# Second block of a two-block transformer kernel: head norms by one root and one reciprocal, residual rows from the norm's rows, context masks on TensorE

## The chip, the cores and the metric

The kernel runs on one core of a Trainium2 chip. The metric is the device time of one execution in microseconds. All arithmetic is fp32. Times named as places (1401.62, say) are microseconds from the start of the profiled span.

## What is computed

Two transformer blocks of two layers each run one after the other over 256 tokens of width 1024. The first has differential attention, a convolution and a mixture of 16 experts, and ends each layer with a layer norm (gain `ln2_g`, bias `ln2_b`). Its output `x` goes into the second block, which the change touches. There 256 context tokens run beside the 256 tokens; the last layer no longer updates the context. The part that matters, cut:

```python
h = rms_norm(x, g_mix[l]) * (1 + sc1) + sh1          # tokens; the same for the context
qa, ka, va, fb, qc, kc, vc = jnp.split(h @ w_in, ...)
qa = rms_norm(qa.reshape(b, l, 6, 64), q_norm)       # head norm: only qa and ka
ka = rms_norm(ka.reshape(b, l, 2, 64), k_norm)
qa, ka, qc, kc = rope of each                        # tokens only
o = concat([global_attention(qa, ka, va, ctx),       # all 512 keys
            fourier_mix(fb),
            window_attention(qc, kc, vc, ctx, sink)]) # |key - query| <= 128, context keys, a sink logit
x = x + gt1 * (o @ w_out[l])
x = x + gt2 * swiglu(...)
```

`rms_norm` over a head is y / sqrt(mean of y squared over 64 channels + 1e-6), times a gain.

## The kernel before, in words

`build` writes one instruction stream per engine by hand: SP loads weight tiles of 2 MB into a ring of six slots, PE (TensorE) multiplies, ACT (ScalarE) and DVE (VectorE) read PSUM. Engines wait for one another on counting semaphores; each engine's order is the order of its program text, so an instruction that waits holds everything behind it on that engine. PSUM has eight banks of 128 x 512.

The first block keeps its rows token-major in `acc`. At the end of its last layer DVE's `row_norm` and ACT's `row_norm` normalise the halves of the rows (L2172, L1635), PE turns them in `turned_rows`, and DVE and ACT write the turned chunks, with gain and bias, into `X` (feature-major, L2179, L1642). PE then multiplies the context's half of the first projection (`context_chunk`) and sums the squares of `X`; DVE's `rms(T, 4, 0, 8, 4)` and ACT's `modulate` make the normalised `h2`.

The second block's loop over the layers `l` (0 and 1) begins on PE with the projection: twelve chunks `n` of 128 output features, each 8 products of 128x128 by the tokens (256 columns, or 512 for chunks 3, 8 and 9 in layer 1). Chunks 0 to 2 are the six qa heads in pairs, 3 is ka, 4 is kc, 5 to 7 are qc, 8 and 9 the values, 10 and 11 the Fourier input. ACT copies each into `pj` and squares chunks 0 to 3 into `squares_h` (L2004). Behind chunk 4 PE sums the squares over each head's 64 channels: `norm_sums` with the block matrix `mean_h`, a 128x128 matrix, once for each of the four chunks, into banks 4 and 5 in turn. The sum comes out copied onto all 64 partitions of its head. DVE adds eps and moves it to SBUF (`variance`, L2085), ACT takes the root (L1622), and DVE takes the reciprocal (`inverse`, L2090) and multiplies (L2997), chunk after chunk: four reciprocals of 128x512 in layer 0. Then DVE rotates chunks 0 to 7 (L3002, L2079, L3005), and signals `s_rope` after chunks 3 and 7.

In layer 0 only, PE turns the tokens' half of `X` back into rows (16 transposes into banks 2, 3, 6 and 7), and ACT copies them into `XR`, the same memory seen as residual rows (L2025).

The attention loop goes over units `(kind, hp, qb, ...)`: kind 0 is global, kind 1 banded; `hp` a pair of heads; `qb` a block of 128 queries. Blocks 0 and 1 are tokens and see 512 keys (four blocks, 1024 columns for the pair), blocks 2 and 3 are context queries and see 256. Layer 0 has 24 units, layer 1 has 12 (no context queries). Step `s` on PE: scores of unit `s` as two products of 64 rows each (after the exponentials of unit s - 2), transposes of the probabilities of unit s - 2 (L1548), the product with the values of unit s - 3. On DVE: the mask addition for banded token queries (L3024, PSUM in place), the negated row maximum (L3027), for kind 1 the sink's part (L3030 and L3032), then reciprocal and scaling of unit s - 1 (L3040, L3044) and the copy of the heads of unit s - 3 (L3054). On ACT: the copy of the transposes (L2039), two exponentials with row sums (L2044) and for kind 1 one exponential of the two sink columns (L2047). Two Fourier steps stand at units 0 and 1. The order in which one PE unit is built:

```python
for par in range(2):
    ins = mm(banks[:, SCORE_BANKS[s % 2] + par, 0:n * P], pj[r, Q_AT[kind] + hp, qb * P:qb * P + P],
             keys[r, k0 * P:(k0 + n) * P], start=True, stop=True)
ins.then_inc(s_scores, 1)
```

Every matrix product of the kernel goes through the helper `mm` (L556), all DMAs of weights through `tile` (L387).

## Time and profile before

| | |
|---|---|
| median of three executions | 2317.36 us (2317.27 to 2323.43) |
| profiled execution, its own time | 2318.68 us |
| its span in the profile | 2317.0 us |
| mean granted TensorE clock | 0.986 of full |
| busy: PE, DVE, ACT, POOL | 2229.0, 1186.2, 448.6, 3.5 us |
| second block, layer 0, projection to last unit | about 1339 to 1482 us |
| second block, layer 1, the same | about 1960 to 2068 us |

A timeline row gives the start, the duration (of a run of equal instructions taken together), the engine, the line, the operation, its operands, the count, and in brackets how long the engine sat idle before it and what ended that. A matrix product in fp32 appears as two records. An engine whose busy share is high is not by that the bound: where another engine's instruction stands between its own, that one is.

### The profile page before, as it was taken

What the parts mean: (1) busy time and instruction counts of PE and PEld (TensorE: products, weight loads), DVE (VectorE), ACT (ScalarE), POOL (GpSimd) and SP (SyncE); (2) the same over time, 40 slices, a digit from 0 to 9 for tenths busy, and PEclk for the clock granted to TensorE, in tenths of its full rate; (3) what the DMA queues carried; (4) which work ended last, traced back from release to release, by engine and by line L of the source; (5) the groups of instructions that cost most, each with busy time, mean ns of one, the idle gap of its engine ahead of it and who ended that gap; (6) DMA issues with size and microseconds to landing.
All of it is one profiled execution on the core that took longest, in us unless ns stands there. A gap on an engine that the chain in (4) does not pass through costs nothing.

```text
span 2317.0 us, 24671 instructions
## 1 busy us (share of the span) xinstructions
PE 2229.0 (96%) x9725; PEld 1399.2 (60%) x9725; DVE 1186.2 (51%) x1983; ACT 448.6 (19%) x1013; POOL 3.5 (0%) x23
## 2 busy tenths in 40 slices
PE   8999999999989999999999998899999999998998
PEld 7755445544357754445444785678888887554453
DVE  3755874211157267752111357765556433687666
ACT  1001402211111014022111225320000102352010
POOL 0000000000000000000000000000000000000000
PEclk9999999999999999999999999999999999999999
DMA  8345844799953459346999520002212124403340
GB/s 337 146 175 224 363 172 173 306 423 428 428 229 146 151 201 412 118 168 272 423 428 427 231 92 18 1 1 102 81 73 87 59 92 172 155 10 145 136 172 18
DMA packets 35983, 451.41 MB, mean 195 GB/s; under 512 B 5160, under 2 KB 7066, under 8 KB 8474
## 3 DMA queue, kind: packets, MB, share of 16 engines
q1 hardware_dynamic: 32992, 447.63, 47.7%
q10 hardware_dynamic: 2874, 2.17, 0.3%
q8 instruction: 81, 1.33, 0.2%
q14 instruction: 36, 0.29, 0.0%
HBM read 448.73 MB, written 1.05 MB: 194 GB/s over the span
## 4 chain that ended last, share of the span: by engine, by line
PE 77%; DMA 10%; DVE 8%; DVEq 2%; issue 1%; ACT 1%; SPq 0%; ACTq 0%
PE banks L556 74%; DMA ring<-in_w_exp_up 9%; PE banks L1548 1%; DVE tiny L3027 1%; DVEq L2091 1%; PE banks L707 1%; DVE tiny L2370 1%; DMA ring<-in_w_in 1%; DVE arena L2384 1%; DVE arena L2090 1%; DVE arena L3044 0%; DVE arena L2079 0%; DVE ring L2116 0%; DVE banks L2367 0%; DVE ring L2825 0%
## 5 line engine op out<-in xcount | busy, mean ns | idle before, releaser
L556 PE MATMUL banks<-ring,arena 128*64 128x512 f32 (+2 forms) x3290 | 966.2, 554 | 18.6 <-DMA ring<-in_w_exp_up 5.8
L556 PEld LDWEIGHTS banks<-ring,arena 128*128 128x128 f32 (+1 forms) x3290 | 446.8, 167 | 506.7 <-issue 473.6
L556 PE MATMUL banks<-arena 128*128 128x128 f32 (+6 forms) x1568 | 239.7, 346 | 13.6 <-ACT arena L2044 6.9
L556 PE MATMUL banks<-X,ring 128*128 128x256 f32 x1024 | 224.1, 381 | 1.8 <-DMA ring<-in_w_in 1.2
L556 PEld LDWEIGHTS banks<-X,ring 128*128 128x128 f32 x1024 | 195.8, 192 | 30.9 <-issue 3.3
L556 PEld LDWEIGHTS banks<-arena 128*128 128x128 f32 (+2 forms) x1568 | 154.5, 176 | 72.3 <-issue 31.5
L556 PE MATMUL banks<-arena,ring 128*128 128x256 f32 (+1 forms) x736 | 178.0, 399 | 2.4 <-ACT arena L1873 2.3
L556 PEld LDWEIGHTS banks<-arena,ring 128*128 128x128 f32 x736 | 139.6, 190 | 36.3 <-issue 17.3
L2215 DVE TENSOR_TENSOR arena<-arena,banks 128x512 f32<-128x512 f32 x16 | 11.0, 687 | 258.2 <-ACT arena L1696 258.2
L556 PE MATMUL banks<-ring 128*128 128x256 f32 x616 | 137.0, 380 | 0.0
L2116 DVE TENSOR_TENSOR ring<-ring 128x2048 f32<-128x2048 f32 (+1 forms) x56 | 119.7, 2138 | 18.0 <-ACT arena L1658 12.5
L556 PEld LDWEIGHTS banks<-ring 128*128 128x128 f32 x616 | 117.3, 190 | 16.0 <-issue 0.5
L2825 DVE TENSOR_TENSOR ring<-ring 128x2048 f32<-128x2048 f32 (+2 forms) x40 | 85.3, 2132 | 32.7 <-PE banks L556 15.0
L556 PE MATMUL banks<-ring,X 128*128 128x512 f32 x192 | 85.1, 593 | 0.3 <-ACT wsums L1614 0.3
L556 PE MATMUL banks<-arena,wsums 128*128 128x256 f32 x320 | 72.3, 379 | 0.0
L556 PEld LDWEIGHTS banks<-arena,wsums 128*128 128x128 f32 x320 | 60.9, 190 | 8.1
L556 PE MATMUL banks<-ring,wsums 128*128 128x256 f32 (+1 forms) x224 | 64.2, 441 | 0.3 <-DVEq L2117 0.3
L556 PEld LDWEIGHTS banks<-ring,X 128*128 128x128 f32 x192 | 36.3, 191 | 43.6 <-issue 43.5
L2198 DVE TENSOR_TENSOR arena<-arena,banks 128x512 f32<-128x512 f32 x64 | 43.9, 686 | 33.7 <-PE banks L556 33.7
L2218 DVE TENSOR_TENSOR arena<-arena,banks 128x512 f32<-128x512 f32 x16 | 11.0, 688 | 96.8 <-PE banks L556 96.8
L1614 ACT ACTIVATE arena<-banks 128x256 f32<-128x256 f32 (+1 forms) x60 | 26.0, 439 | 173.7 <-PE banks L556 170.2
L2321 DVE SCALAR_TENSOR_TENSOR arena<-banks,sinT 32x256 f32<-32x256 f32 x128 | 53.8, 420 | 1.7
(351 smaller groups left out, 1925.5 us busy)
## 6 DMA issues: line engine op xcount, KB each, us to landing
ring<-in_w_in SPq DMA_DIRECT2D x38, 2048.0 KB, 12.2
ring<-in_w_exp_gate SPq DMA_DIRECT2D x32, 2048.0 KB, 13.5
ring<-in_w_exp_up SPq DMA_DIRECT2D x32, 2048.0 KB, 16.6
ring<-in_w_exp_down SPq DMA_DIRECT2D x32, 2048.0 KB, 11.8
ring<-in_w_ada SPq DMA_DIRECT2D x24, 2048.0 KB, 10.9
ring<-in_w_ffn SPq DMA_DIRECT2D x22, 2048.0 KB, 7.6
ring<-in_w_out SPq DMA_DIRECT2D x8, 2048.0 KB, 13.1
ring<-in_w_down SPq DMA_DIRECT2D x8, 1408.0 KB, 6.9
```

Of the source, the lines that this page charges most:

```text
L556: ins = nc.tensor.matmul(out, weights, moving, start=start, stop=stop)
L707: ins = nc.tensor.transpose(bank[b][:, i * P:i * P + P], s_, ident[:])
L1548: ins = nc.tensor.transpose(banks[:, TURNED + par, k * P:k * P + P], probs2[s % 2][:, par, k * P:k * P + P], ident[:])
L1614: done(fn(dst, take()[:, 0:n], func, scale=scale))
L2090: v.reciprocal(dst, dst)
L2091: drain()
L2116: tt(out_, a, b, ALU.subtract)
L2198: done(tt(part_, part_, bank[(7, 4)[i % 2]][:], ALU.add))
L2321: ins = stt(tmp2[o], b[i, 0:T], scale, sinT[i], ALU.mult, ALU.mult)
L2370: v.tensor_reduce(tiny[:, o:o + 2], banks[:, b:b + 2, 0:n * P], AX_X, ALU.max, negate=True) .then_inc(s_max, 1)
L2384: ins = stt(p_[:, 0, :], p_[:, 1, :], tiny[:, o + 6:o + 7], p_[:, 0, :], ALU.mult, ALU.add)
L2825: tt(out_, a_, b_, sub)
```

## The change

Three parts, all in the second block.

**Head norm.** `mean_h` goes. Two small constant matrices come in with the rope tables (`memT[:, 7]`): `head_pick`, 128x32, whose first two columns average over the two heads of a chunk, and `head_spread`, 128x128, which copies rows 32n and 32n + 1 onto the 64 partitions of each head. Behind chunk 4 PE sums the squares of chunk i with `head_pick` into partitions 32i to 32i + 31 of bank 4, all four chunks into one bank. DVE adds eps once, ACT takes one root, DVE one reciprocal (in layer 1 over two areas: 128x256, and 32x256 for the context columns of chunk 3). Behind chunk 6 PE waits for `s_head_inv` and spreads the inverse with four products of 32 rows, chunk i into bank 4 + i; DVE multiplies straight out of these banks.

**Residual rows.** The 16 transposes and 4 copies of layer 0 go. ACT loads `ln2_g` and `ln2_b` of the last layer of the first block, copied onto 128 partitions (two DMAs of 512 KB) into ring slot 5. DVE multiplies `acc` by the gain before the second block's first norm, and adds the bias into `XR` after it.

**Masks and sink.** In layer 0 PE adds the mask of banded token queries to the scores: two more products of `ident` by the mask block (128 columns) that accumulate onto them. In layer 1 DVE still adds it. In both layers DVE no longer prepares the sink's exponent; ACT takes exp(sink + bias) in two instructions of one column in place of one instruction of two.

The diff, cut:

```diff
-        mean_h = sb("mean_h", [P, P])
+        ln_gain, ln_bias = ring[:, 5, 0:D], ring[:, 5, D:2 * D]
+        rows_gained = ring[:, 5, 2 * D:2 * D + TC * D].rearrange("p (a d) -> p a d", a=TC)
+        head_spread, head_pick = memT[:, 7, 0:P], memT[:, 7, P:P + 32]
...
-                    sp.dma_start(memT[:, 4:7, :], a["dft_channels_rope"]).then_inc(s_tables2, 16)
+                    sp.dma_start(memT[:, 4:8, :], a["dft_channels_rope"]).then_inc(s_tables2, 16)
...
+        def head_areas(l):
+            return ((0, P, 0, 2 * T),) if tokens2(l) > T else ((0, P, 0, T), (96, P, T, 2 * T))
+        head_roots = squares_h[:, 0, :]
...
                         if n == 4:
+                            free(4)
                             for i in range(4):
+                                pe.wait_ge(s_square, C.next("square"))
                                 m = proj_tokens(l, i)
-                                norm_sums([squares_h[:, i, 0:m]], m, mean_h, 4 + i % 2, s_square)
+                                ins = mm(bank[4][32 * i:32 * i + 32, 0:m], head_pick, squares_h[:, i, 0:m],
+                                         start=True, stop=True, more=(i < 3))
+                            full(ins, 4, "dve")
+                        if n == 6:
+                            pe.wait_ge(s_head_inv, l + 1)
+                            for i in range(4):
+                                m, r = proj_tokens(l, i), slice(32 * i, 32 * i + 32)
+                                free(4 + i)
+                                full(mm(bank[4 + i][:, 0:m], head_spread[r, :], head_roots[r, 0:m],
+                                        start=True, stop=True), 4 + i, "dve")
...
-                if l == 0:
-                    for i, b in enumerate((2, 3, 6, 7)):
-                        transposes([X[:, 4 * (i % 2) + j, (i // 2) * P:(i // 2) * P + P] for j in range(4)], b, "act")
...
-                                     keys[r, k0 * P:(k0 + n) * P], start=True, stop=True)
+                                     keys[r, k0 * P:(k0 + n) * P], start=True, stop=not masked)
+                        if masked:
+                            m, c0 = ((causal, P), (behind, 0))[qb]
+                            for par in range(2):
+                                ins = mm(banks[:, SCORE_BANKS[s % 2] + par, c0:c0 + P], ident[:], m[:],
+                                         start=False, stop=True)
...
+                if l == DEPTH - 1:
+                    act.dma_start(ln_gain, a["ln2_g"][l, :].partition_broadcast(P)).then_inc(s_ln_rows, 16)
+                    act.dma_start(ln_bias, a["ln2_b"][l, :].partition_broadcast(P)).then_inc(s_ln_rows, 16)
...
-                for n in range(4):
-                    root(squares_h[:, n, 0:proj_tokens(l, n)])
+                act.wait_ge(s_var, C.next("var"))
+                for r0, r1, t0, t1 in head_areas(l):
+                    ins = fn(head_roots[r0:r1, t0:t1], head_roots[r0:r1, t0:t1], ACT.Sqrt)
+                ins.then_inc(s_sqrt, 1)
...
-                if l == 0:
-                    act.wait_ge(s_full["act"], C.next("full_act", 4))
-                    for i, b in enumerate((2, 3, 6, 7)):
-                        done(nc.scalar.copy(XR[:, i // 2, 2 * (i % 2):2 * (i % 2) + 2, 0:T], row_parts(bank[b][:])))
...
-                            ins = fn(tiny[:, o + 6:o + 8], tiny[:, o + 6:o + 8], ACT.Exp)
+                            for par in range(2):
+                                sink = sinks[:, 6 * l + 2 * hp + par:6 * l + 2 * hp + par + 1]
+                                ins = fn(tiny[:, o + 6 + par:o + 7 + par], sink, ACT.Exp, bias=tiny[:, o + par:o + par + 1])
...
+            dve.wait_ge(s_ln_rows, 32)
+            dve.wait_ge(s_rows_a, 2 * DEPTH * TC)
+            for tc in range(TC):
+                tt(rows_gained[:, tc, :], acc[:, tc, :], ln_gain, ALU.mult)
             for l in range(DEPTH):
                 if l == 0:
                     rms(T, 4, 0, 8, 4)
+                    drain()
+                    for tc in range(TC):
+                        tt(XR[:, tc, :, 0:T], row_parts(rows_gained[:, tc, :]), row_parts(ln_bias), ALU.add)
+                filled()
+                for r0, r1, t0, t1 in head_areas(l):
+                    ins = tsc(head_roots[r0:r1, t0:t1], bank[4][r0:r1, t0:t1], NORM_EPS, None, ALU.add)
+                done(ins)
+                drain().then_inc(s_var, 1)
+                dve.wait_ge(s_sqrt, C.next("sqrt"))
+                for r0, r1, t0, t1 in head_areas(l):
+                    v.reciprocal(head_roots[r0:r1, t0:t1], head_roots[r0:r1, t0:t1])
+                drain().then_inc(s_head_inv, 1)
                 for n in range(4):
                     m = proj_tokens(l, n)
-                    variance(4 + n % 2, squares_h[:, n, 0:m], NORM_EPS, m)
-                for n in range(4):
-                    m = proj_tokens(l, n)
-                    inverse(squares_h[:, n, 0:m])
-                    stt(pj[:, n, 0:m], pj[:, n, 0:m], qk_norm[:, n // 3, l:l + 1], squares_h[:, n, 0:m], ALU.mult, ALU.mult)
+                    filled()
+                    done(stt(pj[:, n, 0:m], pj[:, n, 0:m], qk_norm[:, n // 3, l:l + 1], bank[4 + n][:, 0:m],
+                             ALU.mult, ALU.mult))
...
-                        if kind and qb < TC:
+                        if kind and qb < TC and tokens2(l) == T:
...
-                            stt(tiny[:, o:o + 2], sink, -1.0, tiny[:, o:o + 2], ALU.mult, ALU.min)
-                            drain()
-                            ins = tt(tiny[:, o + 6:o + 8], sink, tiny[:, o:o + 2], ALU.add)
+                            ins = stt(tiny[:, o:o + 2], sink, -1.0, tiny[:, o:o + 2], ALU.mult, ALU.min)
```

## Rows read from the trace of the kernel before

**Rows 1.** The page's chain that ended last, shares by engine.
```profile
PE 77%; DMA 10%; DVE 8%; DVEq 2%; issue 1%; ACT 1%; SPq 0%; ACTq 0%
```

**Rows 2.** Timeline, layer 0, norm of the tokens and head norm.
```profile
1312.03 0.42 DVE L2085 TENSOR_SCALAR arena<-banks 128x256 f32<-128x256 f32 x1 [7.98 <-PE banks L556]
...
1339.46 17.43 PE L556 MATMUL banks<-arena,ring 128*128 128x256 f32 x80
...
1356.73 3.79 PE L556 MATMUL banks<-arena,mean_h 128*128 128x512 f32 x8
...
1357.78 0.69 DVE L2085 TENSOR_SCALAR arena<-banks 128x512 f32<-128x512 f32 x1 [40.19 <-PE banks L556]
...
1358.56 0.63 ACT L1622 ACTIVATE arena<-arena 128x512 f32<-128x512 f32 x1 [1.25 <-DVEq L2086]
...
1360.35 10.96 PE L556 MATMUL banks<-arena,ring 128*128 128x256 f32 x50
...
1361.38 3.35 DVE L2090 RECIPROCAL arena<-arena 128x512 f32<-128x512 f32 x1
...
1377.10 0.75 DVE L2997 SCALAR_TENSOR_TENSOR arena<-arena,qk_norm 128x512 f32<-128x512 f32 x1
...
1377.93 0.42 DVE L3002 TENSOR_TENSOR arena<-arena,memT 128x256 f32<-128x256 f32 x1
```

**Rows 3.** Timeline, layer 0, from the residual transposes to the third unit.
```profile
1385.97 1.96 PE L707 MATMUL banks<-ident,X 128*128 128x128 f32 x16
...
1389.74 1.13 PE L556 MATMUL banks<-arena 64*128 64x512 f32 x4 [1.81 <-DVEq L3012]
...
1401.62 2.35 DVE L3027 TENSOR_REDUCE tiny<-banks 128x2 f32<-128x1024 f32 x2
...
1404.38 1.23 PE L556 MATMUL banks<-arena 64*128 64x256 f32 x4 [6.88 <-ACT arena L2044]
```

**Rows 4.** Windows: stretch, length, busy PE, PEld, DVE, ACT, POOL, clock, DMA.
```profile
1404.30:1408.70 4.40, 4.29 (x16) 2.60 (x17) 3.20 (x8) 2.52 (x7) 0.00 (x0) 0.50 0.00 0
...
1434.00:1439.70 5.70, 3.68 (x34) 1.94 (x30) 5.09 (x16) 3.60 (x10) 0.00 (x0) 1.00 0.00 0
1439.70:1443.60 3.90, 3.80 (x20) 2.50 (x20) 2.57 (x10) 2.38 (x9) 0.00 (x0) 0.56 0.00 0
```

**Rows 5.** Groups by shape on PE, 600 to 1300, products of 32 columns.
```profile
L556 PE MATMUL banks<-ring,cond 128*32 128x512 f32 x192 | 23.1, 599 | 0.0
```

**Rows 6.** Timeline, PE, gathering products of 128 columns in the experts.
```profile
1221.21 3.74 PE L556 MATMUL banks<-arena 128*128 128x128 f32 x32
```

**Rows 7.** Timeline, layer 0, DVE in the first banded units.
```profile
1433.18 0.43 DVE L3024 TENSOR_TENSOR banks<-banks,causal 128x256 f32<-128x256 f32 x1 [0.77 <-PE banks L556]
...
1433.69 1.23 DVE L3027 TENSOR_REDUCE tiny<-banks 128x2 f32<-128x1024 f32 x1
...
1434.99 0.16 DVE L3030 SCALAR_TENSOR_TENSOR tiny<-sinks,tiny 128x2 f32<-128x2 f32 x1
1435.23 0.16 DVE L3032 TENSOR_TENSOR tiny<-sinks,tiny 128x2 f32<-128x2 f32 x1
...
1446.84 0.43 DVE L3024 TENSOR_TENSOR banks<-banks,causal 128x256 f32<-128x256 f32 x1 [0.74 <-PE banks L556]
```

**Rows 8.** Chain in order of time: start, length, what, at the transposes.
```profile
1439.80 1.68 PE banks L1548 x8
```

**Rows 9.** Timeline, layer 1, head sums and first row maximum.
```profile
1981.35 2.80 PE L556 MATMUL banks<-arena,mean_h 128*128 128x256 f32 x8
...
1983.99 17.39 PE L556 MATMUL banks<-arena,ring 128*128 128x256 f32 x64
...
2021.38 1.22 DVE L3027 TENSOR_REDUCE tiny<-banks 128x2 f32<-128x1024 f32 x1 [1.84 <-PE banks L556]
```

**Rows 10.** DMA issues: count, KB each, us to landing; 1255 to 1480, whole span.
```profile
ring<-in_w_out SPq DMA_DIRECT2D x2, 2048.0 KB, 23.6
...
memT<-in_g_final ACTq DMA_DIRECT2D x1, 512.0 KB, 3.5
```

More of the change, by code:

```diff
@@ L479, in _ @@
             g = nc.gpsimd
-            for m, v in ((ident, 0.0), (before, 1.0), (causal, 0.0), (behind, 0.0), (mean_h, 1.0 / 64)):
+            for m, v in ((ident, 0.0), (before, 1.0), (causal, 0.0), (behind, 0.0)):
                 g.memset(m[:], v)
@@ L492, in _ @@
                             pattern=[[1, P]], channel_multiplier=-1)
-            g.drain()
-            g.memset(mean_h[0:64, 64:128], 0.0)
-            g.memset(mean_h[64:128, 0:64], 0.0)
             g.drain()
@@ L2040, in _ @@
                     if s < len(units):
-                        kind, n, o = units[s][0], units[s][4] * P, 8 * (s % 2)
+                        kind, hp, n, o = units[s][0], units[s][1], units[s][4] * P, 8 * (s % 2)
                         act.wait_ge(s_max, C.next("max"))
@@ L3081, in _constants @@
         channels[64 * g:64 * g + 64, 0, P + 64 * g:P + 64 * g + 64] = np.sin(ac)
+    heads = np.zeros((P, 1, 2 * P))
+    for n in range(4):
+        heads[32 * n, 0, 0:64] = heads[32 * n + 1, 0, 64:P] = 1.0
+    heads[0:64, 0, P] = heads[64:P, 0, P + 1] = 1.0 / 64
     inv2 = (10000.0 ** (-np.arange(0, 32, 2, dtype=np.float64) / 32)).astype(np.float32)
@@ L3088, in _constants @@
     return {"inv_freq": inv_freq, "dft_tokens": tokens.astype(np.float32),
-            "dft_channels_rope": np.concatenate([channels, cos, sin], axis=1).astype(np.float32)}
+            "dft_channels_rope": np.concatenate([channels, cos, sin, heads], axis=1).astype(np.float32)}
 IN_2_ORDER = (0, 1, 2, 3, 10, 7, 8, 9, 4, 11, 5, 6)
```

3 lines of the change are left out of this document (added).

## The prediction

> **What bounds the kernel now.** I read the page's chain first. TensorE (PE) carries most of it, VectorE (DVE) 8% [rows 1]. So a change to DVE work pays only where DVE holds PE up. I looked for those places with the timeline of both layers of the second block.
>
> In layer 0 it is the head norm. The DVE instructions run back to back: four reciprocals of 3.35 us, each followed by its product with the head (0.75), and only then the rotation of eight chunks, from 1377.93 to the first row maximum at 1401.62, which is 23.69 us [rows 2, 3]. PE has nothing left at 1397.5 and waits 6.88 us, until 1404.38 [rows 3]. Earlier it waited 1.81 us for the first rotated heads, at 1389.74 [rows 3]. When it resumes, its granted clock is 0.50, the 1.2 GHz level, for 4.4 us [rows 4]. The second place is the banded half of the attention. From the mask at 1433.18 to the transposes at 1439.80, 6.62 us, the chain is DVE's, and PE is busy 3.68 us of 5.7 [rows 4, 7, 8]. In the next 3.9 us the granted clock is 0.56 of full. In layer 1 the head norm binds nothing: DVE waited 1.84 us for PE before its first maximum at 2021.38 [rows 9]. Behind both attentions PE runs on with its weights loaded, so what is saved in either place should reach the end of the span.
>
> **The change part by part.** *Head sums, layer 0.* Four full products with mean_h took 3.79 us, eight records from 1356.73 [rows 2]. The new ones have 32 columns each and go side by side into one bank. The trace has this form: 192 records of 128*32 by 128x512 in 23.1 us, 0.12 each [rows 5]. Eight of them are 0.96 us; one after another they would be 8 x 0.43 = 3.44. I take 1.0, since the form is the same. Then one eps addition (0.69), one root, one reciprocal. From the start of the addition to the start of the root 0.78 us pass, the root takes 0.63, the reciprocal 3.35 [rows 2]. With the sums ready at 1357.8 the inverse is ready at 1362.6. PE meanwhile makes chunks 5 and 6, 32 records of 0.219 us = 7.0 [rows 2], and reaches the spreading products at 1364.75. So the added wait on PE, with the chunks 7 to 11 queued behind it, has 2.2 us to spare and costs nothing; if that cover went, it would cost the excess, once in each layer.
>
> *Spreading.* Four products of 32 rows, 512 columns. No row shows 32-row tiles. The nearest one is the pair of 64-row score products: four records in 1.13 us, where 4 x 0.43 = 1.7 would be the serial time [rows 3]. Bounds: 0.9 us (all four at once) and 3.44 (in turn). I take 1.0, nearer to the pair and to the column tiles. That gives 1365.8. Four products with the heads, now out of PSUM, at 0.75 each end at 1368.8. The rotation starts there and not at 1377.93: **9.1 us earlier**, and I put down 9.0. With both sets serial the sums end at 1360.2, the last spread at 1370.7, the last head product at 1371.5: 6.4 us. For the spread alone the Trainium skill, TensorE: Matmul & The Clock Gate, Part 3, gives a measured 3.07 times for four 32-row tiles; by it an estimate is 3.44 / 3.07 = 1.1 us, and the sum would move by 0.1 us.
>
> Is DVE still the later one? PE needed 25.6 us from chunk 5 (1360.35) to the residual transposes at 1385.97 [rows 2, 3]; now it starts at 1357.75, adds 1.0 and arrives at 1384.4. Scores and Fourier products, 7.8 us (1389.74 to 1397.5), end at 1392.2. DVE's first maximum comes at 1368.8 + 23.7 = 1392.5, and PE resumes 2.76 us later, at 1395.3. DVE still sets it, so the whole 9.0 counts, and PE idles 3.1 us instead of 6.88.
>
> *Residual rows.* 16 transposes on PE (1.96 us) and four copies on ACT go [rows 3]. They lay in front of a wait for DVE of 1.81 us, so by themselves they are worth nothing; they only keep PE ahead of DVE. What comes in is four DVE operations over 1024 columns. At 0.42 us per 256 columns [rows 2] they are at most 1.7 each. Two lie in the 7.98 us idle before 1312.03, two in the 40.19 us idle before 1357.78 [rows 2]. Zero; without that cover, 6.7 us. Two more DMAs of 512 KB each on ACT's queue, issued near 1289 behind weight tiles of 2 MB, and a rope table larger by 128 KB on SP's queue: the same kind of row broadcast landed after 3.5 us on a free queue, the weights of that moment after 23.6 [rows 10]. DVE waits for them at about 1303 with the norm behind it (a rival below). POOL loses three fills at the start, beside a load: zero.
>
> *Clock at the loop's start.* The half-rate stretch of 4.4 us is worth at most 2.2 us. With the idle cut to less than half I take 0.8 of it back; bounds 0 and 1.5.
>
> *Masks, layer 0.* Six units lose the addition with its drain, 1433.18 to 1433.69, 0.51 us, and the second sink operation, 1434.99 to 1435.23, 0.24 [rows 7]. PE gets two 128-column products per unit: 32 such records took 3.74 us, so four are 0.47 [rows 6]. Where DVE is the limit a unit gains 0.75; where the chain runs scores, mask, maximum in line it gains 0.28. DVE would need 5.1 us for the masked pair of units, PE 3.7 + 0.9 = 4.6 with waits between, so both kinds occur; I take 0.4 per unit, **2.4 us**. ACT's sink exponential becomes two of about 0.2 us, in units where the chain doesn't pass through ACT: zero, at worst 0.2 x 12. The clock: 3.9 us at 0.56 lack 1.7 us of PE time [rows 4], and it happened in two of the three head pairs (period 13.66 from 1433.18 to 1446.84, [rows 7]). PE goes from 65% to about 90% in the stretch before. I credit one of the two, 1.6. Together 4.0; bounds 0.5 (masks cost as much as they give) and 7.5.
>
> *Layer 1.* PE bounds it. The sums took 2.6 us, from 1981.35 to 1983.99 [rows 9], and become about 1.0; the spread adds about 1.1: minus 0.5. In turn they would be 2.15 + 2.15, plus 1.7. The inverse is later here (two areas, two reciprocals), about 5.5 us after the sums against 7.0 of PE: no wait. The masks stay; six units lose 0.24 on a chain that is all DVE, 1.4, and the last gains 0.2 of ACT: minus 1.2.
>
> **Sum:** 9.0 + 0.8 + 4.0 + 0.5 + 1.2 = 15.5 us. The profiled execution had 2318.68 (span 2317.0, 1.7 around it), which gives 2303.2; it stands 1.3 above the median 2317.36, and from the median I get 2301.9. I say 2302.
>
> **The rivals.** *Small products run in turn.* The column tiles [rows 5] speak against it for the sums; nothing shows 32-row tiles. Layer 0 gives 6.4, layer 1 costs 1.7 instead of giving 0.5, the rest as above: 6.4 + 0.8 + 4.0 - 1.7 + 1.2 = 10.7, so 2306.7. The Trainium skill, TensorEngine Tiling (Array Packing), Key Properties, says that changing the tiling mode drains TensorE. The sequence around a score product already changes shape in each unit without a visible loss of more than some tenths, so the trace doesn't make much of it; four more changes per layer would be an estimate of under 1 us.
>
> *Masks only move the bound.* PE becomes the limit of the banded units, both clock drops stay, and each mask costs its 0.47 plus a switch of weights. For it: the extra 0.9 us per head pair is PE's own. Against it: the 2 us that PE idles in 5.7 of such a pair today [rows 4]. The mask term falls from 4.0 to 0.5 and the clock at the start from 0.8 to 0: 9.0 + 0.5 + 0.5 + 1.2 = 11.2, so 2306.
>
> *It comes out slower.* DVE's wait for the two broadcast rows stands in front of the norm of layer 0. DVE went idle at 1304.05 and began the norm at 1312.03; PE takes the normalised chunks at 1339.46 [rows 2]. The norm itself is a reciprocal of half of 3.35 us, eight products of 0.42 and a root, some 7 us, so 20 of the 27 us are free, and 4.6 of the idle before. It decides only from a landing at about 1304 + 24.6 = 1328.6, and eats the 15.5 us at 1344, which is 55 us after the issue. Landings of 23.6 us under full load speak against it. With a landing at 1355 the time would be 2328.
>
> *The stages behind do not pass it on.* If PE between the attentions had to wait for something that doesn't shift, most of the gain would return: about 2315. No PE wait on a DMA appears there, so this is small.
>
> **How the numbers follow.** Forecast (small products side by side, masks gain): 0.57. In turn: 0.15. Masks only move the bound: 0.20. Not passed on: 0.05. Slower: 0.03. The likeliest gives 2302, with its own bounds 2297.5 to 2306. To hold 8 in 10 I reach up over the two rivals, to 2309, and down to 2297.5, the larger mask and clock terms. 0.3% is 7 us, about what a measurement of this kernel can tell from no change. Faster by more, under 2310.4, holds in the forecast and nearly all of the first two rivals: 0.90. Within 0.3%: 0.08. Slower: 0.02.
>
> **What would show it.** One reciprocal of 3.35 us per layer-0 norm; the rotation starting near 1369; the first maximum near 1392.5 and PE's idle before it about 3 us; the eight sum records in about 1 us; no PE wait for the inverse; a banded period near 12.3 us instead of 13.66 and a clock of 1.0 in it; no mask addition by DVE before layer 1. Wrong would be: spreading products 0.86 us apart, a PE wait behind chunk 6, DVE idle at the broadcast rows past 1312, or a banded period that stays over 13.

## The result and the profile after

The kernel after took 2305.18 us (median of 6 runs, 2304.08 to 2309.91), the kernel before in the same session 2317.59 (6 runs, 2316.88 to 2323.43). The ratio is 0.9947, 95% interval 0.9933 to 0.9961: 12.4 us faster, between 9 and 15.5. The forecast was 2302, within 2297.5 to 2309. The profiled execution took 2305.35 us, with a span of 2303.5 against 2317.0.

From the page of the kernel after, its span, the busy time of each engine, and the chain that ended last, by engine, beside [rows 1]:

```profile
span 2303.5 us, 24658 instructions
PE 2224.4 (97%) x9749; PEld 1392.7 (60%) x9749; DVE 1166.8 (51%) x1953; ACT 448.1 (19%) x1022; POOL 3.0 (0%) x20
PE 78%; DMA 9%; DVE 7%; DVEq 2%; issue 1%; ACT 1%; ACTq 1%; SPq 0%
```

DVE lost 19 us of work, and its share of the chain fell from 8% to 7%. Where the time came from is read from the timeline. Head norm of layer 0 in the kernel after, against [rows 2, 3]:

```profile
1355.65 1.06 PE L563 MATMUL banks<-arena,memT 128*32 128x512 f32 x8
1356.65 7.17 PE L563 MATMUL banks<-arena,ring 128*128 128x256 f32 x32
1356.79 0.69 DVE L3022 TENSOR_SCALAR arena<-banks 128x512 f32<-128x512 f32 x1 [37.89 <-PE banks L563]
1357.56 0.63 ACT L2031 ACTIVATE arena<-arena 128x512 f32<-128x512 f32 x1 [1.42 <-DVEq L3024]
1358.22 3.35 DVE L3027 RECIPROCAL arena<-arena 128x512 f32<-128x512 f32 x1 [0.74 <-ACT arena L2031]
1363.75 1.14 PE L563 MATMUL banks<-arena,memT 32*128 32x512 f32 x8
1364.91 2.72 DVE L3032 SCALAR_TENSOR_TENSOR arena<-arena,qk_norm,banks 128x512 f32<-128x512 f32 x4 [3.34 <-PE banks L563]
1367.73 0.43 DVE L3038 TENSOR_TENSOR arena<-arena,memT 128x256 f32<-128x256 f32 x1
...
1391.44 2.35 DVE L3063 TENSOR_REDUCE tiny<-banks 128x2 f32<-128x1024 f32 x2
...
1394.19 0.70 PE L563 MATMUL banks<-arena 64*128 64x256 f32 x4 [2.63 <-ACT arena L2064]
1395.36 1.86 PE L1568 MATMUL banks<-ident,arena 128*128 128x128 f32 x8 [0.46 <-DVE arena L3078]
```

One reciprocal stands where four stood. It ends at 1361.6, and PE comes to the spreading products at 1363.75, so DVE waits for PE (3.34 us), not PE for DVE. From the head sums to the first row maximum 35.79 us pass, before it was 44.89. PE still idles, 2.63 us instead of 6.88, and the transposes behind it took 1.86 us where the same eight take 1.09 at full clock (in this profile the granted clock is 0.50 from 1395.5 on, for 3.4 us).

The table is the thread of all that follows. It cuts each profiled execution at the same events: A, the first head-sum product of layer 0; B, the first row maximum; C, the maximum of unit 9, the last dense unit over 1024 columns; D, ACT's table load behind the loop of layer 0; E, the first head-sum product of layer 1; F, its first maximum; G, the maximum of its last unit; H, the table load behind that loop. Each number is the difference of two starts in that kernel's timeline.

```
us                     to A     A-B    B-C    C-D     D-E    E-F    F-G   G-H   H-end
before               1356.73  44.89  23.76  56.15  499.82  40.03  37.63  7.79  250.20
after                1355.65  35.79  23.55  52.60  499.93  39.77  36.44  9.19  250.58
e12_after_again      1357.29  35.81  23.42  52.59  499.95  39.76  36.44  7.83  250.71
e1_heads_only        1356.34  35.80  22.54  56.42  498.48  39.76  37.62  7.79  250.35
e2_masks_dve         1358.68  35.78  24.33  53.57  499.81  39.76  36.44  9.18  250.05
e3_sinks_back        1356.24  35.78  23.42  53.73  497.90  39.76  37.62  7.80  250.15
e4_rows_back         1356.54  35.80  22.54  52.59  500.44  39.76  36.79  9.23  249.91
e5_more_reciprocal   1356.18  36.92  22.53  52.96  498.14  43.24  36.46  9.18  250.19
e6_tail_wait         1358.60  35.79  24.35  51.17  499.93  39.76  36.45  7.25  251.00
e9_pe_busy           1359.88  35.79  22.87  52.61  499.68  39.76  36.45  8.69  250.77
e8_rope_tail         1354.74  29.32  32.88  54.08  499.40  39.76  36.46  7.25  251.51
e10_last_chunk_later 1357.87  32.11  22.97  51.18  500.56  39.76  36.44  7.26  249.95
e11_and_masks_dve    1357.32  32.12  22.97  52.09  498.11  39.76  36.45  7.26  249.32
```

Between before and after, the spans differ by 13.5 us: 9.10 in A-B, 0.21 in B-C, 3.55 in C-D, 0.26 in E-F, 1.19 in F-G, of which 1.40 is lost again in G-H, and the rest (1.08 up to A, minus 0.11, minus 0.38) lies in stretches that differ as much between kernels that are the same there. Up to A the 13 profiles range over 5.1 us, in D-E over 2.7. So differences of 1 us are read from the stages, and the medians serve for the total. A stage can be trusted as far as it came back: the eight profiles with the new head norm and nothing else moved on DVE ahead of B give 35.78 to 35.81 in A-B, and the five with both new parts in the banded half and the old tail (after, e12, e4, e5, e9) give 52.59 to 52.96 in C-D. B-C and G-H did not come back so well, as e12 shows below.

### The profile page after: what moved, and what is told of

Read it like the earlier page. It is cut to its first block, busy times and chain, and to the rows that moved or that the text cites. A ratio compares the mean times of both kernels' runs of the same rounds, so it can differ in the third digit from the quotient of the medians.

```text
span 2303.5 us, 24658 instructions
## 1 busy us (share of the span) xinstructions
PE 2224.4 (97%) x9749; PEld 1392.7 (60%) x9749; DVE 1166.8 (51%) x1953; ACT 448.1 (19%) x1022; POOL 3.0 (0%) x20
## 3 DMA queue, kind: packets, MB, share of 16 engines
q10 hardware_dynamic: 3162, 3.21, 0.5%
## 4 chain that ended last, share of the span: by engine, by line
PE 78%; DMA 9%; DVE 7%; DVEq 2%; issue 1%; ACT 1%; ACTq 1%; SPq 0%
PE banks L563 75%; DMA ring<-in_w_exp_up 9%; PE banks L1568 1%; PE banks L714 1%; DVE tiny L3063 1%; DVE tiny L2392 1%; DVE arena L2406 1%; DVE arena L2101 0%; DVE arena L3078 0%; DVE ring L2138 0%; DVE arena L2112 0%; DVE banks L2389 0%; DVEq L2113 0%; DVEq L2405 0%; PE banks L1089 0%
## 6 DMA issues: line engine op xcount, KB each, us to landing
ring<-in_w_in SPq DMA_DIRECT2D x38, 2048.0 KB, 12.1
ring<-in_w_exp_gate SPq DMA_DIRECT2D x32, 2048.0 KB, 13.5
ring<-in_w_exp_down SPq DMA_DIRECT2D x32, 2048.0 KB, 11.9
```

## The experiments

### The three parts by themselves

**e1: only the head norm.** The kernel before with the new head norm. Against the kernel after, its diff is:

```diff
-masked = kind and qb < TC and tokens2(l) > T
+masked = False
...
-if kind and qb < TC and tokens2(l) == T:
+if kind and qb < TC:
...
+                    for i, b in enumerate((2, 3, 6, 7)):
+                        transposes([X[:, 4 * (i % 2) + j, (i // 2) * P:(i // 2) * P + P] for j in range(4)], b, "act")
...
-                            for par in range(2):
-                                sink = sinks[:, 6 * l + 2 * hp + par:6 * l + 2 * hp + par + 1]
-                                ins = fn(tiny[:, o + 6 + par:o + 7 + par], sink, ACT.Exp, bias=tiny[:, o + par:o + par + 1])
+                            ins = fn(tiny[:, o + 6:o + 8], tiny[:, o + 6:o + 8], ACT.Exp)
...
+                            drain()
+                            ins = tt(tiny[:, o + 6:o + 8], sink, tiny[:, o:o + 2], ALU.add)
```

> The kernel before with the head norm of the kernel after, and nothing else of the change (masks by DVE, sink exponents and residual rows as before). Theory A, the three parts add up: the head norm brings the first maximum 9.1 us forward and layer 1's first maximum 0.3 us, so the time is about 9.5 us under the kernel before (ratio 0.996), and the layer-0 banded stage still takes 56.7 us from the reduce of its first unit to the mix unit. Rival B, the head norm's gain needs the residual rows' move: PE's 16 transposes of the residual rows then stand between its last chunk and unit 0's scores, the first maximum is about 2 us later than in the kernel after, and the gain is 7 us or less. Rival C, it pays only as long as DVE is what ends last: PE's idle time before the third unit would then be gone (under 0.3 us) and PE late.

Median 2307.81 us, ratio to before 0.9955 (0.9938 to 0.9972), so 10.4 us less; that total can't be told from the kernel after's (0.9947), so the other parts are read from stages alone. A-B is 35.80, the same as in the kernel after: all of the 9.1 us is the head norm's, and it needs nothing else. B-C is 22.54, 1.2 better than before. PE in the profile of e1, at the loop's start:

```profile
1391.59 3.72 PE L563 MATMUL banks<-memT,arena 128*128 128x256 f32 x16
1395.24 0.70 PE L563 MATMUL banks<-arena 64*128 64x256 f32 x4
1396.06 1.09 PE L1572 MATMUL banks<-ident,arena 128*128 128x128 f32 x8
```

PE has no wait there that the timeline lists, and all runs at full clock. Rival B is out, and of rival C one half came true: PE's idle time is gone, but PE is not late. C-D is 56.42, as before.

**e4: only the residual rows undone.** The kernel after with the 16 transposes and four copies back, without the broadcast rows.

> The kernel after with the residual rows as before: PE transposes them ahead of the loop over pairs, ACT copies them, no broadcast rows, no row arithmetic on DVE. Theory A, the rows are worth nothing because DVE ends last there: the first maximum stays where it is (35.8 us after the head sums start), PE's idle time before the third unit falls from 2.63 us to about 0.7, and the time is within 0.5 us of the kernel after. Theory B, the same, and with so short a wait the granted clock stays at full speed when PE resumes (1.0 instead of 0.64 over the first 5 us), so that this kernel is about 1 to 1.5 us faster than the kernel after. Rival C: PE's transposes push unit 0's scores behind DVE's rotation; then the first maximum is up to 2 us later and the kernel slower by as much.

Median 2305.79, ratio to before 0.9943 (0.9925 to 0.996): the totals of this kernel and the kernel after can't be told apart. The stages can. PE in the profile of e4:

```profile
1384.53 1.96 PE L714 MATMUL banks<-ident,X 128*128 128x128 f32 x16
1387.75 1.13 PE L563 MATMUL banks<-arena 64*128 64x512 f32 x4 [1.26 <-ACT X L2051]
...
1395.44 0.70 PE L563 MATMUL banks<-arena 64*128 64x256 f32 x4
1396.26 1.09 PE L1572 MATMUL banks<-ident,arena 128*128 128x128 f32 x8
```

The transposes, and a wait of 1.26 us behind them, cost nothing: A-B stays at 35.80, and PE resumes 3.10 us after the first maximum where it was 2.75. B-C is 22.54 against 23.55. In this profile theory B's stage came out, with 1.0 us of the 1 to 1.5; its total is not shown. Taking 2 us of work from PE in front of a wait for DVE made the wait longer, and the slow clock behind it cost 1.0 us, where the work had cost nothing. (Behind such a wait the slow clock comes mostly, not always; see e5 and the last section.)

**e2: layer 0's masks back on DVE**, by the first two edits of e1's diff.

> The kernel after with layer 0's context masks added by DVE as before (no mask products on TensorE). Theory A: the banded stage goes back from 52.6 us to 56.7, with a period near 13.7 us and stretches of it at a granted clock under 1; the time is 4.1 us over the kernel after (ratio to it 1.0018). Rival B: the 4.1 us are mostly the sink's second DVE operation left out and not the masks; then the stage takes under 54.5 us here. Rival C: the clock drops of before were a matter of where the stage began; then the period is 13.0 us at a clock of 1.00 throughout, and the time is 2.4 us over.

Median 2307.52, ratio to before 0.9947 (0.993 to 0.9965). The banded stage is not 4.1 us longer but 1.0 (53.57 against 52.60). Theory A was a miss, and the number of rival B (under 54.5) came out. The windows of the kernel after (stretch, length, busy PE, PEld, DVE, ACT, POOL, granted clock, DMA share, GB/s), one period of the banded units (the four units of one pair of heads) and what comes behind the last:

```profile
1426.80:1438.80 12.00, 10.83 (x97) 7.23 (x96) 9.02 (x29) 9.35 (x28) 0.00 (x0) 1.00 0.01 1
...
1450.80:1454.80 4.00, 2.84 (x28) 1.93 (x28) 3.63 (x11) 2.63 (x9) 0.00 (x0) 1.00 0.01 4
1454.80:1458.80 4.00, 3.20 (x36) 2.23 (x32) 3.06 (x11) 4.00 (x12) 0.00 (x0) 1.00 0.00 2
```

and of e2:

```profile
1429.70:1441.70 12.00, 10.13 (x92) 6.39 (x89) 10.00 (x31) 9.62 (x31) 0.00 (x0) 1.00 0.00 0
...
1453.70:1457.70 4.00, 2.21 (x22) 1.58 (x20) 3.35 (x9) 2.55 (x9) 0.00 (x0) 1.00 0.00 2
1457.70:1461.70 4.00, 4.00 (x25) 2.59 (x22) 2.96 (x12) 2.30 (x7) 0.00 (x0) 0.57 0.02 4
```

With the masks on DVE the period is 11.89 us (maxima at 1429.94, 1441.83 and 1453.72), with them on TensorE 12.12 and 12.10 (1426.58, 1438.70, 1450.80). So the units are faster without the mask products. From C to the last of these maxima e2 takes 34.93 us against 35.81; from there to D 18.64 against 16.79. What it loses is in the last window: a PE wait of 1.79 us, then 4 us in which the granted clock is 0.57 of full, mostly at the lower level.

**e3: the sink's exponent as before**, by the last two edits of e1's diff.

> The kernel after with the sink's exponent as before (one more DVE addition, one ACT exponent of two columns), both layers. Theory A: in layer 1 each banded unit takes 0.24 us more (3.58 against 3.34), 1.2 us up to the last unit's maximum, but the half clock behind it (1.35 us in the kernel after, where 24 products and transposes ran at 0.78 to 0.89 of full clock) goes away, so that the start of the next stage is the same within 0.3 us; layer 0's banded period stays at 12.1. The time is within 0.5 us of the kernel after. Rival B: the clock drops there whatever the sink's form; then layer 1 is 1.2 us longer. Rival C: the split exponent costs ACT more than DVE saves; then this kernel is faster by over 0.5 us, to be seen in layer 0's tail, where PE waited 1.4 us for ACT's sink exponent against 1.1 before.

Median 2308.61, ratio to before 0.9955 (0.9939 to 0.9972). Layer 1 did as theory A says: F-G 37.62 instead of 36.44, G-H 7.80 instead of 9.19, the sum within 0.3 us of the kernel after. Layer 0 did not: its period is 12.58 us, not 12.1, and C-D 53.73; in the total it is 2 us behind the kernel after by the ratios, within their intervals. The four kernels in which both parts vary (all have the new head norm) give, from unit 13's maximum to unit 17's, one period of the banded units, and for the stage:

```
us: one period, C-D   sink as before           sink new
masks on DVE          12.60, 56.42 (e1)        11.89, 53.57 (e2)
masks on TensorE      12.58, 53.73 (e3)        12.12, 52.60 (kernel after)
```

At full clock the move of the masks is worth 0.02 us a period with the old sink, and costs 0.2 with the new one; leaving out the sink's second DVE operation is worth 0.5 to 0.7. Over the stage either part alone gives 2.7 to 2.9 us, and both together 3.8, no more. The period of 12.60 us in e1 was followed by one of 14.15. The windows of e1 show why:

```profile
1426.00:1438.60 12.60, 10.04 (x90) 6.29 (x88) 10.48 (x34) 8.48 (x27) 0.00 (x0) 1.00 0.01 1
1438.60:1446.00 7.40, 5.70 (x39) 3.72 (x38) 5.80 (x17) 4.17 (x13) 0.00 (x0) 0.77 0.00 0
```

Between the first window and the next the granted clock fell, as it did in the kernel before [rows 4]. What goes ahead of it is PE's wait for DVE in front of the transposes, once in each period. In the kernel before, e3, e2 and the kernel after:

```profile
1439.80 1.68 PE L1548 MATMUL banks<-ident,arena 128*128 128x128 f32 x8 [1.71 <-DVE arena L3044]
1430.06 1.09 PE L1568 MATMUL banks<-ident,arena 128*128 128x128 f32 x8 [1.41 <-DVE arena L3078]
1432.73 1.09 PE L1568 MATMUL banks<-ident,arena 128*128 128x128 f32 x8 [1.47 <-DVE arena L3078]
1429.37 1.10 PE L1568 MATMUL banks<-ident,arena 128*128 128x128 f32 x8 [1.17 <-DVE arena L3078]
```

With neither part the wait is 1.70 us or 1.71 (six of them in before and e1, four followed by a drop). With the masks on TensorE alone it is 1.41, with the sink's form alone 1.47, with both 1.17, and behind none of these did the clock fall. So the mask products pay by shortening this wait, and the sink's form shortens the same wait: in the first two periods either is enough to keep the clock up. In the third only the masks are, for e2's wait there is the one of 1.79. That the two gains of 2.7 and 2.9 make only 3.8 together fits this: both contain the clock that either would have kept. For e2 and e3 this rests on one profile each; e11 repeats e2's waits and periods.

### What a wait of PE costs

**e5: one more reciprocal** of 128x512 on DVE, its result unused, ahead of the signal for the inverse roots.

```diff
+                v.reciprocal(squares_h[:, 1, :], squares_h[:, 1, :])
                 drain().then_inc(s_head_inv, 1)
```

> The kernel after with one more reciprocal of 128x512 on DVE (3.35 us, its result unused) ahead of the signal for the inverse roots, in both layers. Theory A, the head norm's new chain is hidden by PE's chunks 5 and 6: the two reciprocals end 9.3 us after the head sums start, PE comes to the spread products at 8.1 us, so PE waits about 1.2 us and the first maximum comes 37.0 us after the sums instead of 35.8; 2.1 of the 3.35 us are cover. Rival B, the chain is what sets the first maximum already: 39.1 us. Rival C, there is more cover than the trace shows, since PE is not what ends last: 35.8 us as before.

One run, 2307.68 us. In layer 0 A-B is 36.92, as theory A has it (37.0): 3.35 us more on DVE cost 1.1, the rest was cover. Layer 1 was a surprise: E-F grew by 3.48 us. PE in the profile of e5:

```profile
1365.39 1.14 PE L563 MATMUL banks<-arena,memT 32*128 32x512 f32 x8 [1.04 <-DVEq L3029]
...
1395.86 0.70 PE L563 MATMUL banks<-arena 64*128 64x256 f32 x4 [2.66 <-ACT arena L2064]
1397.02 1.09 PE L1568 MATMUL banks<-ident,arena 128*128 128x128 f32 x8 [0.46 <-DVE arena L3079]
...
1976.62 1.14 PE L563 MATMUL banks<-arena,memT 32*128 32x256 f32 x8 [1.72 <-DVEq L3029]
1977.69 12.27 PE L563 MATMUL banks<-arena,ring 128*128 128x256 f32 x32
```

and the same 32 products in the kernel after:

```profile
1976.69 10.59 PE L563 MATMUL banks<-arena,ring 128*128 128x256 f32 x32
```

The wait took 1.72 us and the products behind it 1.68 us more, with the granted clock at half for 3.4 us from 1978.4: at a wait like this one, PE can pay twice. In layer 0 the same kernel shows the opposite. Behind its wait of 2.66 us the eight transposes took 1.09 us, at full clock, where they took 1.86 behind 2.63 us in the kernel after.

**e9: products that nobody reads** in two of PE's waits.

```diff
+                            if s == 2 and l == 0:
+                                free(7)
+                                for i in range(16):
+                                    nc.tensor.matmul(bank[7][:, 0:P], ident[:], ident[:], start=True, stop=True)
...
+                            for i in range(12):
+                                nc.tensor.matmul(bank[SCORE_BANKS[s % 2]][:, 0:P], ident[:], ident[:], ...)
```

> The kernel after with matmuls whose result nobody reads put into two of PE's waits: 16 products of 128 columns (about 2.2 us) ahead of the third unit in layer 0, and 12 (about 1.6 us) ahead of the wait behind the last unit in layer 1. Nothing else moves, so this parts the clock from all else. Theory A: the half clock follows from PE's idle time. At the loop's start PE resumes at a granted clock of 1.00 and unit 9's maximum comes 22.5 us after the first, not 23.55; in layer 1 it is 7.8 us, not 9.19, from the last maximum to the table load: 2.4 us in all. Rival B: the added products delay what they stand ahead of as much as the clock gives. Rival C: the clock drops there whatever PE does.

Median 2306.06, ratio to before 0.9941 (0.9926 to 0.9957). The 16 products took 3.73 us and not 2.2, the 12 took 2.94 and not 1.6; I had taken one record for one product, and each product leaves two. So they overfilled both waits. Still, PE in the profile of e9, layer 0 and layer 1:

```profile
1395.63 3.73 PE L1544 MATMUL banks<-ident 128*128 128x128 f32 x32
1399.29 0.70 PE L563 MATMUL banks<-arena 64*128 64x256 f32 x4
1399.92 1.09 PE L1576 MATMUL banks<-ident,arena 128*128 128x128 f32 x8
...
2048.53 2.94 PE L1564 MATMUL banks<-ident 128*128 128x128 f32 x24
2051.31 1.04 PE L1576 MATMUL banks<-ident,arena 128*128 128x128 f32 x8
```

In layer 0 PE came 0.87 us later out of the wait (3.62 after the first maximum, not 2.75) and B-C was 0.68 shorter all the same; in layer 1 G-H fell from 9.19 to 8.69 with 0.9 us of overfilling in it. The trace fits theory A: nothing was changed but that PE had work, and the clock stayed up in both places. It is one profile, and the next run shows that the drop in layer 1 can be missing without any such products, so it does not prove that they kept the clock up. If they did, they cost 1.2 us of the 2.4 that the clock gave (0.33 in B-C over the 22.54 of a stage with no drop, 0.86 in G-H over 7.83).

**e12: the kernel after, again.**

> The kernel after, unchanged, once more. Its profile tells whether the two half-clock stretches (behind the wait of 2.63 us in layer 0, and behind that of 1.79 us in layer 1) come back at the same places. Theory A: both do: 23.5 us from the first maximum to unit 9's, 9.2 us from the last maximum of layer 1 to the table load. Rival B: they depend on something that differs from run to run (e5 had the same wait of 2.66 us in layer 0 and no drop): 22.5 or 7.8 us at one of them. The head sums start anywhere between 1354.7 and 1359.9 us, as in the ten profiles so far.

Median 2305.62, ratio to before 0.9939 (0.9926 to 0.9953), so 14.1 us less than the kernel before in that session (2319.70). Rival B came true for layer 1. The timeline of PE at the step behind the last unit, in the first profile of the kernel after:

```profile
2047.09 1.66 PE L1568 MATMUL banks<-ident,arena 128*128 128x128 f32 x8 [1.79 <-ACT tiny L2069]
2048.68 1.98 PE L563 MATMUL banks<-arena 128*64 128x128 f32 x16
```

in e12:

```profile
2048.62 1.09 PE L1568 MATMUL banks<-ident,arena 128*128 128x128 f32 x8 [1.80 <-ACT tiny L2069]
2049.64 1.09 PE L563 MATMUL banks<-arena 128*64 128x128 f32 x16
```

and in the kernel before:

```profile
2062.33 1.09 PE L1548 MATMUL banks<-ident,arena 128*128 128x128 f32 x8 [1.76 <-ACT tiny L2047]
```

The same program, the same wait, once with the slow clock behind it and once without. So the 1.40 us that the first profile lost in G-H are not there in every execution of the kernel after, and my theory for e3 is not shown. It is not refuted either: of the profiles with a wait of this kind, the drop came in four of the five with the new sink (after, e2, e4, e5; not e12) and in none of the three with the old (before, e1, e3). Whether the sink's form makes it likelier is open. In layer 0 the drop came back (23.42). But how much it costs there varies as well: behind the same wait of 2.63 to 2.67 us B-C took 22.53 us (e5, no drop), 23.42 to 23.55 (after, e12, e3: half clock for 3.4 us) or 24.33 and 24.35 (e2, e6: for 6.8 us).

### A version that beats both

**e6: the wait behind the last unit.** PE waited there for the last unit's exponents in both layers, though only layer 0 needs a score bank at that step, and that is the bank of the unit before.

```diff
-                    elif s == len(units):
-                        pe.wait_ge(s_exp, exped[s - 1])
+                    elif s in fourier:
+                        pe.wait_ge(s_exp, exped[s - 2])
```

> The kernel after, where PE at the step behind the last unit no longer waits for that unit's exponents: in layer 1 it waits for nothing but the probabilities it transposes, in layer 0 (whose Fourier product writes a score bank) for the exponents of the unit before the last, whose bank it is. Theory A, the half clock in layer 1 comes from PE's wait of 1.79 us there: the transposes start about 0.6 us earlier behind a wait of 1.2 us, run at full clock (1.09 us, not 1.66), and from the last unit's maximum to the table load behind the loop it takes 7.2 us instead of 9.19; in layer 0 the wait of 1.36 us goes and the mix unit starts up to 1.3 us earlier: about 3 us in all. Rival B, the clock drops all the same: 8.6 us in layer 1. Rival C, in both tails the next wait (the last unit's probabilities from DVE) takes the place of the one removed: under 0.5 us in all.

Median 2304.62, ratio to before 0.9933 (0.9919 to 0.9946). G-H is 7.25, as forecast (7.2), and C-D 51.17 instead of 52.60. That is 1.43 us in layer 0 and 0.6 in layer 1 beside the clock's 1.4, which e12 shows to be absent in some executions. In the medians this doesn't stand out from the kernel after.

**e8: half of the rotation in the loop**, with e6's edit.

```diff
+                ahead = 8 if l == 0 else 16
+                for n, piece in pieces[:ahead]:
+                    turned_by_place(n, piece)
+                later = dict(zip(range(1, 9), pieces[ahead:]))
...
+                    if s in later:
+                        turned_by_place(*later[s])
```

> As the kernel without the tail's wait, and in layer 0 the rotation of chunks 4 to 7 (11.9 us on DVE) is done in eight pieces behind the steps 1 to 8 of the loop over pairs instead of ahead of it. Theory A, DVE's rotation is what still makes PE idle at the loop's start: the first maximum comes with unit 0's scores (about 29.3 us after the head sums instead of 35.8), PE has no wait of 2.63 us before the third unit and no half clock behind it (3.6 us earlier at unit 9's maximum), and the eight pieces of 1.3 us fit into the 2.6 us that DVE is free per dense unit: 3.6 us beside what the tail gives. Rival B, the pieces delay the maxima and exponents of units 2 to 8, PE waits for them, and more than half of it is given back. Rival C, PE, and not DVE, ends last there: nothing is gained but the clock's 1.0 us.

Median 2307.25, ratio to before 0.9948 (0.9934 to 0.9961). The first maximum came at 29.32 us, as expected, and unit 9's 62.2 us after the sums instead of 59.3. Rival B, and more than the whole gain. A window of e8:

```profile
1410.00:1420.00 10.00, 6.75 (x57) 3.91 (x54) 9.28 (x24) 5.52 (x15) 0.00 (x0) 0.94 0.00 1
```

and the worst of PE's waits in it, from the timeline:

```profile
1419.37 1.97 PE L1568 MATMUL banks<-ident,arena 128*128 128x128 f32 x8 [3.21 <-DVE arena L3088]
```

DVE is full, and PE waits for it in the middle of the loop.

**e10: only the last chunk later.** PE's idle time asks for 2.63 us. So only chunk 7 and the swapped keys (3.6 us) move into the loop, in four pieces, with e6's edit.

```diff
+                for n in range(7):
...
+                later = {} if l else {2: 0, 3: 1, 6: 2, 7: 3}
...
+                    if s in later:
+                        last_by_place(later[s])
```

> The kernel after with the tail's wait moved as in e6, and of DVE's rotation only what PE's idle time asks for put into the loop in layer 0: chunk 7 (2.7 us) and the copies of the swapped keys of the second kind (0.86 us), in four pieces of some 0.9 us behind steps 2, 3, 6 and 7. Theory A: the first maximum comes 32.2 us after the head sums instead of 35.8, PE has no wait ahead of the third unit and no half clock, unit 9's maximum comes 55.7 to 56.5 us after the head sums instead of 59.3, and with the tails' 3.4 us the kernel is about 6.5 us faster than the kernel after (ratio to before about 0.992). Rival B, DVE is so nearly full in the dense units that even these pieces make PE wait, as the eight of e8 did (62.2 us): then the first gain is under 1 us. Rival C: the wait only moves to another unit and the half clock with it.

Median 2300.01 us (5 runs, 2298.43 to 2302.31), ratio to before 0.9914 (0.99 to 0.9927). A-B is 32.11 and A-C 55.08, better than the 55.7 that I gave as best; PE in e10:

```profile
1390.05 3.72 PE L563 MATMUL banks<-memT,arena 128*128 128x256 f32 x16
1393.70 0.70 PE L563 MATMUL banks<-arena 64*128 64x256 f32 x4
1394.34 1.09 PE L1568 MATMUL banks<-ident,arena 128*128 128x128 f32 x8
```

No wait that the timeline lists, no slow clock. The pieces cost 0.4 us inside the loop (B-C 22.97, where 22.54 is a stage with no drop). It is 5.6 us under the kernel after, run beside it in the same session (2305.62).

**e11: and the masks on DVE.**

> e10 with layer 0's context masks added by DVE as before. With the sink's new form DVE has room for the masks: e2 had a banded period of 11.88 us with them on DVE, against 12.10 with them on TensorE, and lost 1.85 us only in the tail, where PE had its longest wait and then ran at a granted clock of 0.57. Theory A: with the tail's wait moved the clock stays up, and the layer-0 stage from unit 9's maximum to the table load is 0.3 to 0.9 us shorter than in e10: the masks on TensorE are worth only what they do for the clock. Rival B: the clock drops in the tail as in e2, and the stage is about 1 us longer than in e10. Rival C: it drops inside the banded units too, as in the kernel before, and the stage is 3 to 4 us longer.

Median 2297.82 (4 runs, 2295.6 to 2298.5), ratio to before 0.9903 (0.9887 to 0.9918). The stage C-D says rival B: 52.09 against 51.18. The periods are 11.90 and 11.89, as in e2, and then the tail of e11 shows the drop again:

```profile
1450.46 1.09 PE L1568 MATMUL banks<-ident,arena 128*128 128x128 f32 x8 [1.79 <-DVE arena L3099]
1451.48 1.82 PE L563 MATMUL banks<-arena 128*64 128x128 f32 x12
1453.23 1.97 PE L1568 MATMUL banks<-ident,arena 128*128 128x128 f32 x8
```

The wait is for DVE's scaling, which e6's edit doesn't touch. That the median is 2.2 us lower than e10's has no cause in the stages that differ: D-E, where the two are alike, was 2.45 us shorter, within what it varies by. The intervals of the two overlap, though three of e11's four executions lie below all five of e10's; which is the better one stays open, and both beat the kernel after.

## Why the prediction was right or wrong

**Head norm, layer 0 (9.0): right.** Measured 9.1, in e1 by itself. The sums took 1.06 us (1.0), the spread 1.14 (1.0), with bounds of 3.44 for both. The trace agrees with the 1.1 us worked out from the Trainium skill, TensorE: Matmul & The Clock Gate, Part 3. No drain of more than 0.2 us shows at the change of tiling, of which the Trainium skill, TensorEngine Tiling (Array Packing), Key Properties speaks: the chunk's products start 1.07 us after the spread began, and all four at once would be 0.86 (two records of 0.43 in a row). The rival of products in turn is out. The cover was there as named, 2.2 us: e5 spent 3.3 and paid 1.1.

**Residual rows (0): the cover was there, one step was wrong.** DVE in the kernel after:

```profile
1305.38 2.36 DVE L3012 TENSOR_TENSOR ring<-arena,ring 128x1024 f32<-128x1024 f32 x2 [3.54 <-issue]
...
1310.87 0.42 DVE L2107 TENSOR_SCALAR arena<-banks 128x256 f32<-128x256 f32 x1 [2.08 <-PE banks L563]
```

The products with the broadcast row started at 1305.38, when the second row landed (issued at 1288.11, 17.2 us before). DVE idled 3.54 us for it, and the variance behind them still waited 2.08 us for PE, where it had waited 7.98. The slower case, which needed a landing at 1328.6, was far off. But the step "they only keep PE ahead of DVE" took being ahead for worthless. Without the transposes PE idles 2.63 us instead of none listed, and in the profile of the kernel after loses 1.0 us to the clock (against e4).

**Clock at the loop's start (0.8): oversized.** B-C fell by 0.21 (0.34 in e12); over the six profiles with this wait it is 23.60 in the mean, 0.16 less than the one profile before. I took the clock's loss as going with the length of the idle time. 2.63 us of it were enough to bring the lower level back, in five of the six profiles that have this wait.

**Masks, layer 0 (4.0): size nearly right, reason in good part wrong, so the size is luck in part.** C-D fell by 3.55. I had split it into 2.4 from the work taken off DVE and 1.6 from one clock drop of two. The period did fall to 12.1 (12.3 foreseen), but by the sink's operation, in all twelve banded units and not in six, and by the clock, which stayed at 1.00 in all three periods. The mask addition that moved to TensorE gives nothing at full clock (12.60 against 12.58 with the old sink, 11.89 against 12.12 with the new); it pays only by the shorter wait. The step that failed is the gain of 0.75 per unit "where DVE is the limit", of which 0.51 is the mask addition: at full clock no period showed it. The other case of the prediction, 0.28, in which the mask is worth 0.51 less 0.47, is the one that came. The rival "masks only move the bound" had that part right, and was wrong that the drops would stay.

**Layer 1 (0.5 and 1.2).** The sums and the spread gave 0.26, where 2.6 for the old sums less 1.0 for the new and 1.07 for the spread would be 0.5. The rest lies in the 64 chunk records behind the sums: 17.22 us in one piece before (1983.99 to 2001.21), 7.10 and 10.43 around the spread after. Why they take 0.3 more was not tried. The sink gave 1.19 in F-G, as worked out; the first profile loses 1.40 behind it by a clock drop that e12 did not have. The prediction had no term for a drop there, and whether the new sink makes one likelier is open.

**The sum.** By stages the change is worth 9.1 + 0.2 + 3.55 + 0.26 + 1.19 = 14.3 us against 15.5, and the medians say 12.4, or 14.1 in e12's session. The difference of 1.9 lies within the interval, and in stretches that vary by more from run to run; the drop in G-H, 1.4 us, is of the same size. The total is right with two terms that were not: it does not test a term of 1 us.

## What to carry to other kernels

Where PE waits for another engine on and off, first ask what the clock does behind each wait: work that stands in front of a wait may cost nothing where it is, and an edit is credited wrongly if its stage changed level. Take such a stage from more than one profile. Test parts one by one, for two edits that shorten the same wait share its gain. To end a wait, move little more of the late engine's work than the wait is long (3.6 us for a wait of 2.63 gained, 11.9 us lost), into places where that engine has room.

## What the hardware did that I had not expected

A wait of 1.72 us on PE was followed by products that took 1.68 us more than at full clock (e5, layer 1). The drop is not settled by the length of the wait: behind 1.76 to 1.80 us in layer 1 it came in four kernels (after, e2, e4, e5) and not in four (before, e1, e3, e12), of which two are the same program; behind 2.63 to 2.67 us in layer 0 it came in after, e2, e3, e6 and e12, and not in e5. Behind 1.79 us at the end of layer 0's loop it came both times (e2, e11). Behind 1.70 or 1.71 us in the banded units it came in four of six (before, e1), behind 2.03 and 3.21 both times (e8), and behind 1.81 in layer 0 of before it did not. Behind 1.22 or 1.23 us in layer 1 (e6, e8, e10, e11) it did not come, nor behind any other wait of 1.0 to 1.5 us between 1300 and 1500 and between 1955 and 2080 us, 55 in the thirteen profiles with these four. What decides between the two from 1.7 us on is open. And the same code up to A took from 1354.74 to 1359.88 us in the ten profiles that have it, which is wider than most of the terms disputed here.
